# A transformer layer on one core: tile 3's opening half ahead of the transposes in the output projection's last column block, and a weight slab rounded one tile earlier

## The reference

```python
x = x + merge_heads(attention) @ w_out         # (512,1024) @ (1024,2048)
h = x * rsqrt(mean(x * x, axis=-1) + eps) * norm_ffn
gu = h @ w_gate_up                             # (512,2048) @ (2048,11264)
x = x + (silu(g) * u) @ w_down
```

## Time and profile before

| | |
|---|---|
| time, median of 3 runs | 1750.96 us (1750.95 to 1751.29) |
| the profiled execution, its time | 1749.86 us |
| its span | 1748.0 us |
| PE busy | 1719.6 us, 98% of the span |
| DVE busy | 1198.3 us, 69% |
| ACT busy | 789.2 us, 45% |
| POOL busy | 203.1 us, 12% |
| TensorE's granted clock, mean | 0.997 of full speed |
| the last column block and the seam | about 401 to 450 us of the span |

### The profile page before, as it was taken

One profiled execution on the slowest core, in us unless ns is written; L12 is line 12 of the kernel. 1 busy time (PEld: TensorE's weight loads), 2 busy tenths in 40 slices (PEclk: granted clock), 3 DMA queues, 4 the chain that ended last, 5 costly groups with the idle time before them and its releaser, 6 DMA issues.

```text
span 1748.0 us, 24616 instructions
## 1 busy us (share of the span) xinstructions
PE 1719.6 (98%) x8928; PEld 1469.8 (84%) x8928; DVE 1198.3 (69%) x1274; ACT 789.2 (45%) x956; POOL 203.1 (12%) x294
## 2 busy tenths in 40 slices
PE   8999999999999999999999999999999999999997
PEld 6888888887888888888888888888887888888886
DVE  6433323335877777777777777777778978878886
ACT  5222322234444554455445554454444544444454
POOL 3000000002101111111111111111111100000044
PEclk9999999999999999999999999999999999999999
DMA  7332323252347677777777677777787886876854
GB/s 235 79 97 74 95 72 96 72 202 64 92 127 197 175 180 201 201 187 180 190 190 183 175 183 206 198 176 187 186 241 214 248 242 200 249 188 186 262 146 136
DMA packets 306563, 297.77 MB, mean 170 GB/s; under 512 B 9424, under 2 KB 258512, under 8 KB 300752
## 3 DMA queue, kind: packets, MB, share of 16 engines
q1 hardware_dynamic: 288848, 224.71, 41.7%
q0 software_dynamic: 15264, 66.07, 19.6%
q10 hardware_dynamic: 2400, 6.29, 1.0%
HBM read 203.72 MB, written 27.26 MB: 132 GB/s over the span
## 4 chain that ended last, share of the span: by engine, by line
PE 92%; DVE 3%; issue 1%; ACT 1%; DMA 1%; POOL 1%; ACTq 0%; DVEq 0%; POOLq 0%
PE ps L2044 29%; PE ps L1830 22%; PE ps L2095 21%; PE ps L2050 15%; PE ps L2028 2%; PE ps L2033 1%; DVE tmp L1344 1%; DVE split L1658 1%; PE ps L1843 1%; DMA raw<-raw 1%; DVE down_slot L1667 0%; DVE hT L1332 0%; POOL xres L872 0%; DVE split L1524 0%; DMA xres<-in_x_dram 0%
## 5 line engine op out<-in xcount | busy, mean ns | idle before, releaser
L1084 ACT ACTIVATE split<-raw 128x1024 fp32r<-128x1024 f32 x295 | 312.2, 1058 | 344.8 <-DVE raw L1535 110.8
L1524 DVE TENSOR_TENSOR split<-raw,split 128x1024 fp32r<-128x1024 f32 x295 | 360.6, 1223 | 141.4 <-ACT split L1084 137.3
L2095 PE MATMUL ps<-split,operand_hi 128*128 128x512 f32 x1232 | 381.3, 390 | 7.2 <-issue 3.2
L1830 PE MATMUL ps<-hT,split 128*128 128x512 f32 (+1 forms) x1392 | 288.5, 368 | 0.8 <-DVE split L1325 0.8
L2095 PEld LDWEIGHTS ps<-split,operand_hi 128*128 128x128 f32 x1232 | 231.1, 188 | 58.1 <-issue 6.2
L1830 PEld LDWEIGHTS ps<-hT,split 128*128 128x128 f32 x1392 | 241.3, 189 | 43.5 <-issue 1.0
L2044 PE MATMUL ps<-hT,split 128*128 128x512 f32 x984 | 246.4, 392 | 0.5 <-ACT split L1084 0.5
L2095 PE MATMUL ps<-split,operand_lo 128*128 128x512 f32 x616 | 239.7, 389 | 0.0
L1183 ACT ACTIVATE split<-down_slot 128x2048 fp32r<-128x2048 f32 (+1 forms) x84 | 148.6, 1774 | 183.8 <-PE ps L2095 89.2
L2044 PEld LDWEIGHTS ps<-hT,split 128*128 128x128 f32 x984 | 177.0, 189 | 32.4 <-issue 0.7
L1658 DVE TENSOR_TENSOR split<-down_slot,split 128x2048 fp32r<-128x2048 f32 (+1 forms) x84 | 177.2, 2109 | 26.4 <-ACT split L1183 22.8
(11 more groups left out here) (164 smaller groups left out, 1885.0 us busy)
## 6 DMA issues: line engine op xcount, KB each, us to landing
raw<-in_ffn_w_gate_up_dram SPq DMA_DIRECT2D x172, 512.0 KB, 4.8
raw<-raw POOLq DMA_DIRECT2D x82, 512.0 KB, 4.5
down_slot<-in_ffn_w_down_dram SPq DMA_DIRECT2D x32, 1024.0 KB, 7.0
raw<-in_fox_w_in_dram SPq DMA_DIRECT2D x24, 1024.0 KB, 5.7
a_sums<-pack SPq DMA_DIRECT2D x22, 1024.0 KB, 6.3
down_slot<-down_slot POOLq DMA_DIRECT2D x16, 1024.0 KB, 8.0
operand_raw<-a_sums SPq DMA_DIRECT2D x28, 512.0 KB, 6.4
down_slot<-in_ffn_w_down_dram SPq DMA_DIRECT2D x16, 768.0 KB, 6.5
```

What stands on the lines that cost most here:

```text
L1084: nc.scalar.activation(ring(r, 0, n), source, ACT.Copy).then_inc(t_hi, 1)
L1524: nc.vector.tensor_tensor(ring(r, 1, n), source, f32(ring(r, 0, n)), ALU.subtract).then_inc(t_lo, 1)
L1830: ins = nc.tensor.matmul(bank, stationary(sp, t), moving(mp, t), start=first and t == tiles[0] and (sp, mp) == PASSES[0], stop=last and t ...
L2095: ins = nc.tensor.matmul(banks[:, tile, :], operand[e][part][:, i, tile * P:(tile + 1) * P], down_ring(dn, part_of_t, e)[:, i * BANK:(i + ...
```

## The change

Three lists are edited.

```diff
@@ ACT
             for cb in range(NC - 1):
                 for tb in range(NT):
+                    if tb == NT - 1:
+                        split_hi(wo.plus(2 * cb + 3))
                     square(NT * cb + tb + 1, cb, tb, ps[:, YB[cb % 2][tb], :])
-                split_hi(wo.plus(2 * cb + 3))
                 if cb < NC - 2:
                     split_hi(wo.plus(2 * cb + 4))
             last = NC - 1
             for tb in range(NT):
-                if tb == NT - 1:
-                    split_hi(wo.plus(2 * NC))
                 square(NT * last + tb + 1, last, tb, ps[:, YB[last % 2][tb], :])
                 if tb == NT - 1:
                     split_hi(wo.plus(2 * NC + 1))
...
                 if tb < NT - 1:
                     scale(1, tb)
+                if tb == 1:
+                    split_hi(wo.plus(2 * NC))
             take_hT(1, NT - 1)
@@ DVE
             for tb in range(NT):
-                if tb == NT - 1:
+                if tb == 2:
                     split_lo(wo.plus(2 * NC))
                 add(NT * cb + tb + 1, cb, YB[cb % 2][tb], tb)
@@ PE
-            for tb, part in ((0, 0), (1, 0), (0, 1), (1, 1), (2, 0), (2, 1), (3, 0), (3, 1)):
+            for tb, part in ((0, 0), (1, 0), (0, 1), (1, 1), (2, 0), (3, 0), (2, 1), (3, 1)):
                 if part == 1 and tb == 2:
                     turn(1, 0)
                 half(NC - 1, part, tb)
```

## The result

| | before | changed |
|---|---|---|
| median of 11 runs of each | 1750.47 us | 1754.75 us |
| lowest to highest | 1748.69 to 1752.10 | 1752.79 to 1759.13 |
| ratio, 95% interval | | 1.0026 (1.0018 to 1.0033) |

The changed kernel is slower by 0.26%, 4.3 us by the medians. One execution differs from the next by 3 us and more, as much as the effect. So I compare within the traces, by the length of the **seam**: from the start of add 3 of column block 2 to the start of turn 3. It is read from one profiled execution of each kernel. Before, that is 446.10 - 406.64 = 39.46 us.

What follows compares the result with a forecast made beforehand. PE, busy 98% of the span, was taken to bound the kernel. Turn 3 3.7 us later plus 1.1 us of low clock made 4.8, so 1750.96 + 4.8 = 1755.8 us, range 1753.8 to 1758.0.

Steps and rivals of the forecast that it cites:

- Part 1: In blocks 0 to 2 ACT rounds the second slab before tile 3's square; claimed gain 0.56 us, before 412.28.
- Turn 0 late by 2.2: On PE, (3,0) goes before turn 0, which starts at about 422.8 instead of 420.62, 2.2 us later.
- Norm 1 takes the long 3.19: On DVE, norm 1 starts 0.32 us behind POOL's multiply and so takes 3.19 us, not 2.35.
- The rival in which it gets ahead of POOL: Norm 1 on DVE starts before POOL's multiply and takes 0.84 us less: +2.9 us, 1753.9; chance 13%.
- Slab 8 ahead of add 2: DVE's low part of slab 8 takes 2.20 us before add 2, which starts at 431.85, 5.21 us later.
- The stall: PE idle before turn 2 for some 3.6 us, then 1.2 more after 4 transposes.
- The chain's size: Late work on tile 2 delays the gate product; turn 3 starts at 449.8 instead of 446.10, 3.7 us later.
- The clock: After the stall PE falls to 1.2 GHz; turn 2's last 12 transposes cost 1.1 us more, bounds 0 and 1.7.
- The bound of 1.7: Upper bound of the clock's cost: half of the 3.5 us low stretch at the start, all on PE's work.
- The case with two such stretches: Rival: low clock lasts over turn 2 and the gate product: 3.7 + 2 x 1.7 = +7.1, 1758.1; chance 10%.
- The choice between the row at the kernel's start and the one at 1320 us: Whether the clock falls after the stall (start row, +4.8) or stays at 2.4 GHz (1320 us, +3.7, chance 22%).
- The sum: Whole kernel: 3.7 + 1.1 = 4.8 us slower, 1755.8 us, 0.27%; chance of this forecast 45%.

Runs made afterwards that it cites:

- filled kernel: The changed kernel plus 12 matmuls that nobody reads, ahead of turn 2; time ratio 1.0019 (1.0010 to 1.0028) to the kernel before.
- slab 9 first: The kernel before with Part 1, and ACT also rounds slab 9 ahead of the last block's last square; time ratio 0.9994 (0.9985 to 1.0003).
- slab 7 only: The kernel before with Part 1 alone, PE's order and slab 8 as before; time ratio 0.9998 (0.9989 to 1.0007).
- slab 8 only: The kernel before with Part 1 and slab 8 rounded one tile earlier, PE's order as before; time ratio 1.0045 (1.0031 to 1.0059).

## Why the prediction was right

- **Part 1**: 0.56 us predicted, 0.57 measured alone.
- **Turn 0 late by 2.2**: it started 424.75 - 1.98 = 422.77; 422.8 predicted.
- **Norm 1 takes the long 3.19**: it started 0.29 us behind POOL's multiply (428.42 against 428.13; 0.32 expected) and took 3.16 us to the slab's start. The rival in which it gets ahead of POOL did not come in the changed kernel, nor in any other profile with (3,0) moved.
- **Slab 8 ahead of add 2**: add 2 late by 5.17, predicted 5.21. Taken out, the stall at turn 2 falls from 3.73 to 1.52; put behind add 2, to 2.40.
- **The stall**: 3.73 and 1.02, predicted 3.6 and 1.2. The waits of 0.76 and 0.64 are gone, as predicted. The working overlooked a fifth wait in that stretch: 0.15 us ahead of turn 0's last chunk at 422.24, put down to POOL, so all that could be won there was 2.75 us and not 2.6. It is gone in the changed kernel as well.
- **The chain's size**: 3.7 predicted. The filled kernel, with the same add 2 and turn 2 and the product at 2.4 GHz, has 42.80 - 39.46 = 3.3. The 0.3 or 0.4 too much is turn 2: from the second chunk's start to the product I took 1.55 us from the earlier trace rows (426.77 to 428.32); where all chunks are ready it is 439.88 - 438.60 = 1.28.
- **The clock**: this term was too small. I took 1.1 us, turn 2's last 12 transposes. In both profiles of the changed kernel the low clock reached into the product. In the first it cost 0.9 us on the transposes (443.87 - 441.40 = 2.47 against 1.55) and 1.5 on the 72 matmuls (10.16 us to turn 3 against 8.70), 2.4 in all; against the filled kernel 2.6. The bound of 1.7 was too low as well, as it took one stretch like that at the start. The case with two such stretches, which I gave 10%, is what these two profiles show in kind, though at +5.95 in the seam and not at +7.1. So turn 3 came at 454.03 - 1.98 = 452.05 and not at 450 to 451, and the low clock lasted to 445.2 and not to 443. The choice between the row at the kernel's start and the one at 1320 us could not be made from one trace: with slab 9 first, whose code at 1320 us is that of before, the clock was at 0.50 from 1321.2 to 1324.4 us, right behind that sparse stretch, while in the trace of before it stayed at 1.00 from 1300 to 1350 us.
- **The sum**: 1755.8 us predicted, 1754.75 measured. Of the loss, 4.8 predicted, 4.3 by the medians, 5.95 and 6.05 in the two profiled seams. That 4.8 comes so near to 4.3 is in part luck: the chain was 0.3 too long and the clock's share 1.3 to 1.5 too small in the executions that can be read, and when the changed kernel was timed again the medians were 6.6 apart. The first median lies below the traces, and the 11 runs hold others with less low clock (mean granted clock 0.996 at 1752.79 us, 0.992 at 1759.13), which would explain it. Runs of equal mean clock differ by less: at 0.995, four changed runs average 1754.4 us and eight of the kernel before, timed beside the experiments, 1751.8. That is 2.6 apart, not far from the chain's 3.3; the clock is on record to three digits only, so this is rough. How the low clock of each unprofiled run divides between the seam and the start is not seen.

The reason why the change is slower, in a sentence: it frees PE of two waits for weight slabs, 0.6 us at no cost (part 1) and 0.8 us by taking the cover from tile 2's chain and putting work in front of that chain, and the chain was already on the path.

## What to carry to other kernels

Where an engine is busy 98% of the time, ask of every work that is moved what it covered where it was; (3,0) was the cover of a chain of 7.5 us that goes through four engines. In this kernel an early operand was worth something where the instruction that makes it went into an idle spot of its engine's list: on DVE behind add 2, or, for slab 9, on ACT ahead of the square. In front of the chain's first step it made that step late by its full length, 2.2 us. And where single runs scatter as much as the effect, the distance between two marks in the trace (here repeated to 0.1 us, in two profiles) tells what the time does not.

## What the hardware showed

A stall can cost TensorE more than its length. In the changed kernel, after 3.73 us of idle time, 4 transposes and 1.02 us more, the granted clock was 1.2 GHz (0.50 over 443 to 446 us, with PE fully busy, and part of the next stretch); this added 2.4 to 2.6 us to a late chain of 3.3. It also fell once, in the filled kernel, after waits of only 0.64 and 1.02 us around turn 1, the same waits after which it stayed up in the changed kernel. So in such a place one run may have the low clock and the next not. The TensorE page of the Trainium skill (TensorE: Matmul & The Clock Gate, HAM oscillation) speaks of slow restarts after long idle gaps; the trace agrees for the 3.73 us, and for the shorter waits it shows that a fall can come there too.

All nine traces together: in the six with (3,0) moved or slab 8 early the clock fell once between 415 and 450 us, in the three others (before, slab 7 only, slab 9 first) it stayed at 1.00. So the fall goes with the waits that the late chain makes. What a fall costs does not follow the length of the wait. With slab 8 only, PE waited 7.48 us, and the clock fell at 441.2, still in the wait and ahead of turn 2; the product then had 9.10 us, against 10.32 in the changed kernel.

Much of the scatter of the runs goes with the same clock. In the first 30 us, which are the same code in all nine kernels, it was never low in two traces (filled, slab 9 first), and add 3 of block 2 starts at 405.79 and 405.88. In the two traces with the most of it (changed, slab 8 only: mean 0.83 over these 30 us) it starts at 408.62 and 409.09.
